# A fused pair of decoder blocks on one core: the opening rearranged into quarters of 256 features

## The reference, cut to what matters

```python
mod_x = split(silu(c) @ w_ada + b_ada, 6)           # shift and gain rows for the tokens: sh1, sc1, ...
mod_c = split(silu(c_ctx) @ w_ada[:, :2*D] + ..., 2) # the same for the context tokens
hx = rms_norm(x, norm1) * (1 + sc1) + sh1            # 256 x 1024
hc = rms_norm(ctx, norm1) * (1 + mod_c[1]) + mod_c[0]
ak, av, gk, gv, lrf, lrb, aq, gq, go, ga, gg = split(hx @ w_in)      # products with slices of w_in
ak_c, av_c, gk_c, gv_c, lrf_c, lrb_c = split(hc @ w_in[:, :CTX_COLS])
```

## Time and profile before

| | |
|---|---|
| time, median of 3 (lowest to highest) | 910.68 us (909.92 to 911.31) |
| profiled execution: its own time, its span | 910.58 us, 908.7 us |
| mean granted TensorE clock | 0.998 |
| PE busy | 889.8 us (98%) |
| DVE busy | 623.5 us (69%) |
| ACT busy | 479.5 us (53%) |
| DMA | 162.11 MB, 178 GB/s in the mean |

### The profile page before, as it was taken

The page is one execution under the profiler, slowest core; times in us unless marked ns, Lnnn a source line. Parts: engine busy times, 40 slices in busy tenths (PEclk is TensorE's granted clock), DMA queues, the critical chain, the costliest instruction groups (busy, mean ns, idle before and its releaser), DMA issues.

```text
span 908.7 us, 14136 instructions
## 1 busy us (share of the span) xinstructions
PE 889.8 (98%) x5128; PEld 761.3 (84%) x5128; DVE 623.5 (69%) x992; ACT 479.5 (53%) x759; POOL 12.6 (1%) x25
## 2 busy tenths in 40 slices
PE   7999999999999999999999999999999999999996
PEld 2688888887788888889999998997888999999985
DVE  2668779779878978775555558767777855555575
ACT  3737545656656566474444444544655744444454
POOL 0200000000000000000000000000000000000001
PEclk9999999999999999999999999999999999999999
DMA  9955212335446877636555558353434665555531
GB/s 360 351 175 171 80 55 93 95 110 153 154 145 230 263 247 263 213 133 230 187 188 185 185 185 270 101 185 117 162 118 161 228 225 197 191 194 183 189 120 47
DMA packets 45376, 162.11 MB, mean 178 GB/s; under 512 B 5615, under 2 KB 5759, under 8 KB 45328
## 3 DMA queue, kind: packets, MB, share of 16 engines
q1 hardware_dynamic: 42896, 155.73, 51.0%
q0 software_dynamic: 1296, 4.02, 1.6%
q10 hardware_dynamic: 1136, 1.70, 0.5%
HBM read 160.39 MB, written 1.05 MB: 178 GB/s over the span
## 4 chain that ended last, share of the span: by engine, by line
PE 80%; DVE 10%; ACT 4%; DMA 3%; issue 2%; POOL 0%; SPq 0%; POOLq 0%; DVEq 0%; ACTq 0%
PE bank L704 67%; DVE w_lo L1706 3%; DMA arena<-in_early 2%; PE bank L971 1%; PE bank L888 1%; ACT w_hi L1271 1%; PE bank L878 1%; ACT arena L1350 1%; PE bank L1173 1%; PE bank L991 1%; PE bank L986 1%; PE bank L1204 1%; DVE small L1736 1%; DMA raw<-in_stream 1%; PE bank L895 1%
## 5 line engine op out<-in xcount | busy, mean ns | idle before, releaser
L1706 DVE TENSOR_TENSOR w_lo<-raw,w_hi 128x1024 fp32r<-128x1024 f32 x244 | 288.0, 1219 | 156.0 <-ACT w_hi L1271 155.3
L1271 ACT ACTIVATE w_hi<-raw 128x1024 fp32r<-128x1024 f32 x244 | 245.2, 1050 | 195.4 <-PE bank L704 163.8
L704 PE MATMUL bank<-w_hi,act_lo 128*128 128x512 f32 (+1 forms) x728 | 294.1, 404 | 0.3 <-DVE w_lo L1706 0.2
L704 PE MATMUL bank<-w_lo,act_hi 128*128 128x512 f32 (+1 forms) x728 | 282.7, 388 | 0.0
L704 PE MATMUL bank<-w_hi,act_hi 128*128 128x512 f32 (+1 forms) x728 | 282.3, 388 | 0.0
L704 PE MATMUL bank<-act_lo,w_hi 128*128 128x256 f32 x640 | 183.0, 286 | 1.1 <-DVE act_lo L1706 0.6
L704 PE MATMUL bank<-act_hi,w_hi 128*128 128x256 f32 x640 | 181.0, 283 | 0.0
L704 PE MATMUL bank<-act_hi,w_lo 128*128 128x256 f32 x640 | 181.0, 283 | 0.0
L704 PEld LDWEIGHTS bank<-w_lo,act_hi 128*128 128x128 f32 x728 | 136.7, 188 | 29.2
L704 PEld LDWEIGHTS bank<-w_hi,act_lo 128*128 128x128 f32 x728 | 137.1, 188 | 26.6 <-issue 1.7
L704 PEld LDWEIGHTS bank<-w_hi,act_hi 128*128 128x128 f32 x728 | 137.2, 188 | 25.8 <-issue 1.2
(11 more groups left out here) (253 smaller groups left out, 768.7 us busy)
## 6 DMA issues: line engine op xcount, KB each, us to landing
raw<-in_stream SPq DMA_DIRECT2D x278, 512.0 KB, 4.4
arena<-in_early SPq DMA_DIRECT2D x14, 512.0 KB, 12.0
res<-in_x ACTq DMA_DIRECT2D x1, 1024.0 KB, 9.0
raw<-in_early SPq DMA_DIRECT2D x2, 512.0 KB, 13.6
arena<-in_ctx SPq DMA_DIRECT2D x1, 1024.0 KB, 13.5
res<-in_x POOLq DMA_DIRECT2D x1, 1024.0 KB, 7.9
arena<-in_norm_final POOLq DMA_DIRECT2D x1, 512.0 KB, 4.1
arena<-in_ple_b POOLq DMA_DIRECT2D x1, 512.0 KB, 5.0
```

Of the source, the lines that this page charges most:

```text
L704: last = pe.matmul(o, left, right, start=start and m == 0, stop=stop and m == 2, skip_group_check=shared)
L1271: return act.activation(o, i, ACT.Copy)
L1706: return dve.tensor_tensor(o, x, hi.bitcast(F32), ALU.subtract)
```

## The change

The opening goes by quarters of 256 features. Early units are laid out anew: four units a quarter, each 512 rows x 256 columns, of shift columns or gain columns. A unit is now four matmuls of 256 columns, one in each strip (step `strip`), before two of 512 in two strips. Per quarter q: four `strip` steps, `flip` (the turn of the tokens' two blocks of 128 features, 4 transposes of 128x128), `row`, `columns` (now 4 transposes of 128x128 instead of products with a strip matrix, which is gone), `mods` (now with a small reduction over the strips by VectorE), `raise` (gain and shift of 128x256 on each of ScalarE and VectorE, then the rounding to `act_hi`), `lower` (`act_lo`), and the gk and gq products of these features, in pieces of 6 matmuls: 24 for gk and 24 for gq a quarter.

In the list of tiles gq and gk change places, so that kv takes gq's slot and its units can be rounded once gq's products are done. gq's second group, which stood behind lr, is now in the quarters; gk of the context and lr come after them. ada 6 stood in front of kv in the stream of raw units and in the steps; it now comes after kv's four units. The context's squares are split in two steps. SP's queue is written by hand up to unit 7, and x comes through it, first, in two halves. The ring of early units is 7 slots, before 7 and two raw buffers.

```diff
-MIXER1 = ["gk", "gq", "kv", ...
+MIXER1 = ["gq", "gk", "kv", ...
-EARLY = (0, 2, 1, 3)
+RING = (1, 4, 5, 6, 7, 8, 0)
@@ mixer1_plan
-    p = Plan([("early",), ("norm", "n0"), ("row", 0), ("row", 1), ("mods", 0), ("turn", "n0", (0, 1))] + cuts("gk", (0, 1))
...
-    p.steps += p.group("gk", 2) + [("evac", "gk", 2), ("prepare",), ("mm", "gk", 3, 0), ("ada", 6, 0), ("mm", "gk", 3, 1),
-                                   ("ada", 6, 1), ("mm", "gk", 3, 2), ("ada", 6, 2), ("mm", "gk", 3, 3), ("evac", "gk", 3),
-                                   ("ada", 6, 3)]
-    p.steps += [("mm", "lr", 0, 0), ("round", "kv", 0), ("cut", "kv", 0), ("evac", "lr", 0), ("round", "kv", 1),
-                ("cut", "kv", 1), ("mm", "gq", 1, 0), ("gate", 0), ("round", "kv", 2), ("mm", "gq", 1, 1), ("log_decay", 0),
-                ("cut", "kv", 2), ("round", "kv", 3), ("mm", "gq", 1, 2), ("cut", "kv", 3), ("mm", "gq", 1, 3),
-                ("evac", "gq", 1)]
+    bring = lambda q: [("row", q), ("columns", q), ("mods", q)]
+    p = Plan([("early",), ("norm", "n0")] + strip(0, 1, 2, 3) + [("flip", 0)] + bring(0) + [("round", "gk", 0), ("raise", 0),
+              ("cut", "gk", 0), ("lower", 0)] + cut("gq", 0)
+             + both("gk", 0, 0) + strip(4, 5) + [("flip", 1)] + both("gk", 1, 0) + strip(6, 7) + cut("gk", 1)
+             + [("row", 1)] + mm("gq", 0, 0, 0) + [("columns", 1), ("mods", 1), ("raise", 1), ("lower", 1)]
+             + mm("gq", 0, 0, 1) + both("gq", 1, 0) + cut("gq", 1))
...
+    p.steps += (both("gk", 0, 2) + [("squares", "n1", 0)] + strip(12, 13) + [("flip", 3)] + both("gk", 1, 2) + cut("gk", 3)
+                + [("squares", "n1", 1)] + strip(14) + mm("gq", 0, 2, 0) + [("norm", "n1")] + strip(15) + [("row", 3)]
+                + mm("gq", 0, 2, 1) + [("columns", 3), ("mods", 3), ("raise", 3), ("lower", 3)] + both("gq", 1, 2)
+                + cut("gq", 3))
+    p.steps += (both("gk", 0, 3) + [("evac", "gk", 0), ("turn", "n1", (0, 1))] + both("gk", 1, 3) + [("evac", "gk", 1)]
+                + [("turn", "n1", (2, 3))] + both("gq", 0, 3) + [("evac", "gq", 0)] + both("gq", 1, 3) + [("evac", "gq", 1)])
+    sides = [[], [("prepare",)], cut("kv", 0), [("evac", "gk", 2)] + cut("kv", 1), [("evac", "lr", 0)] + cut("kv", 2),
+             [("gate", 0)] + cut("kv", 3), [("ada", 6, 0)], [("log_decay", 0), ("ada", 6, 1)], [("evac", "gk", 3)]]
+    for step, side in zip(p.group("gk", 2) + [("mm", "lr", 0, 0)] + p.group("gk", 3), sides):
+        p.steps += [step] + side
+    p.steps += [("ada", 6, j) for j in (2, 3)]
@@ TensorE
+            def strip(p):
+                part, unit = p % 4, early_unit(p).rearrange("p (k n) -> p k n", k=4)
+                half = slice(T * (part % 2), T * (part % 2) + T)
...
+                pe.wait_ge(ada_in[p], 16)
+                for k in range(4):
+                    last = pe.matmul(psum[6][32 * k:32 * k + 32, half], silu_m[:, 4 * (part // 2) + k, :], unit[:, k, :],
+                                     start=(part == 0), stop=(part >= 2), skip_group_check=True)
+                last.then_inc(strips_done, 1)
+            def columns(q):
...
+                for b in range(4):
+                    c = q * NC + b * P
+                    last = pe.transpose(psum[7][:, b * P:(b + 1) * P], ada_row[:, c:c + P], ident)
+                last.then_inc(row_turned, 1)
@@ VectorE
+                elif kind == "raise":
...
+                    dve.wait_ge(turned, q + 1)
+                    dve.tensor_scalar(turn_y[:, q].rearrange("p k t -> p (k t)")[:, 0:T], psum[4][:, 0:T],
+                                      gain[:, 2 * q:2 * q + 1], shift[:, 2 * q:2 * q + 1], ALU.mult, ALU.add).then_inc(turn_y_dve, 1)
+                elif kind == "lower":
...
+                    dve.wait_ge(turn_hi, q + 1)
+                    lo_part(act_lo[:, 2 * q:2 * q + 2, 0:T], ...).then_inc(turn_done, 1)
@@ SyncE
-            for p in range(EARLY_UNITS):
-                if p >= 9:
-                    sp.wait_ge(strips_done, p - 8)
-                sp.dma_start(early_unit(p), a["early"][p]).then_inc(ada_in[p], 16)
...
+            for t in range(TT):
+                sp.dma_start(res[:, t, :], tokens("x")[:, t]).then_inc(x_in[t], 16)
+            for p in range(4):
+                early(p)
+            for u in range(3):
+                unit(u)
+            for p in range(4, 8):
+                early(p)
+            unit(3)
+            unit(4)
+            for p in range(8, 12):
+                early(p)
+            context(0)
+            unit(5)
+            unit(6)
+            context(1)
+            for p in range(12, 16):
+                early(p)
+            unit(7)
```

More of the change, by code:

```diff
@@ new lines, in mixer1_plan @@
+    p.steps += (both("gk", 0, 1) + strip(8, 9) + [("flip", 2)] + both("gk", 1, 1) + strip(10, 11) + cut("gk", 2)
+                + [("row", 2)] + mm("gq", 0, 1, 0) + [("columns", 2), ("mods", 2), ("raise", 2), ("lower", 2)]
+                + mm("gq", 0, 1, 1) + both("gq", 1, 1) + cut("gq", 2))
+    p.steps += (both("gk", 0, 2) + [("squares", "n1", 0)] + strip(12, 13) + [("flip", 3)] + both("gk", 1, 2) + cut("gk", 3)
+                + [("squares", "n1", 1)] + strip(14) + mm("gq", 0, 2, 0) + [("norm", "n1")] + strip(15) + [("row", 3)]
+                + mm("gq", 0, 2, 1) + [("columns", 3), ("mods", 3), ("raise", 3), ("lower", 3)] + both("gq", 1, 2)
+                + cut("gq", 3))
@@ new lines, in flip @@
+            def flip(q):
+                if q == 0:
+                    pe.wait_ge(first_in, 16 * N_FIRST)
+                    pe.wait_ge(norm_ready, TT)
+                for c in range(2):
+                    if q > 0:
+                        pe.wait_ge(turn_y_act if c else turn_y_dve, q)
+                    for t in range(TT):
+                        last = pe.transpose(psum[4 + c][:, t * P:(t + 1) * P], x_norm[:, t, (2 * q + c) * P:(2 * q + c + 1) * P],
+                                            ident)
+                last.then_inc(turned, 1)
@@ L1223, in _ @@
                     mm(*step[1:])
-                elif kind == "early":
-                    early()
+                elif kind == "strip":
+                    strip(step[1])
+                elif kind == "flip":
+                    flip(step[1])
                 elif kind == "columns":
                     columns(step[1])
-                elif kind == "turn" and step[1] != "n0":
+                elif kind == "turn":
                     turn(*step[1:])
@@ L1828, in turn @@
                     ins.then_inc(turn_y_dve, 1)
-                    if name == "n0" and b == 2:
-                        split_unit("gk", 2)
                     if name == "n2" and b == 0:
@@ L2300, in _ @@
                     evac(step[1], step[2])
-                elif kind == "cut" and step[1:] != ("gk", 2):
+                elif kind == "cut":
                     split_unit(step[1], step[2])
@@ L2327, in _ @@
                 elif kind == "mods":
[L2328 to L2330 removed]
+                    q = step[1]
+                    at = slice(2 * q, 2 * q + 2)
+                    if q == 0:
                         dve.wait_ge(first_in, 16 * N_FIRST)
[L2332 removed]
+                    dve.wait_ge(row_turned, q + 1)
+                    sums = stat[:, 7, 8:16].rearrange("p (a c v) -> p a c v", a=2, c=2)
@@ L2453, in laid_out @@
     units = [parts[n][j] for n, j in CUTS]
-    early = [parts[f"ada{i}"][j] for i in EARLY for j in range(4)]
+    early = []
+    for q in range(4):
+        for rows in (0, NC):
+            for c in (T * q, D + T * q):
+                w = inp["w_ada"][0][rows:rows + NC, c:c + T].reshape(4, P, T).transpose(1, 0, 2)
+                early.append(w.reshape(P, 4 * T))
     def columns(v):
```

202 lines of the change are left out of this document (105 added, 97 removed), and 3 rows, old and new, of the table p.

## The result

The changed kernel takes 918.11 us (median, 916.50 to 918.85), the kernel before 910.30 beside it: a ratio of 1.0082, 95% interval [1.0070, 1.0095]. It is slower by 0.8%, outside the 0.2% that the prediction took as no change, and 4.1 us above the forecast of 914.0; the upper end of the range, 918.0, is just missed. The profiled execution took 916.50 us, its span is 914.7. A second profile of the same changed kernel (first experiment) has a span of 916.1, so two executions are read here.

What follows compares the result with a forecast made beforehand. TensorE, busy 98% of the span, was taken as the bound. The opening seemed to give 1.8 us at kv, but VectorE's chain delays the scans, making it 910.6 + 3.4 = 914.0 us; range 908.6 to 918.0.

Steps and rivals of the forecast that it cites:

- Step 1: Landing of early data: 1.33 us per 512 KB, last early unit in at 38.9 us, before about 30.
- step 2: First gk/gq product of the opening: at 17.0 us against 28.59 before, TensorE waiting from 13.5.
- Step 3: Quarters on TensorE: 9.6 us each, quarter 3 begins at 47.5, gk and gq done at 56.1; TensorE paces, not the stream.
- wait for `lower`: In each quarter TensorE waits 0.5 us for VectorE's `lower`; 0.7 more in the third quarter.
- slow start: After the early gap, TensorE's first products run at half pace for a while: 1.0 us more.
- Step 4: From the quarters to the scans: scans at 78.4, 3.2 us later; TensorE idles some 5 us, end moves 3.2 to 3.5.
- cover of tile 6: Before, ada 6's eight VectorE passes ran under gk of the context and lr; claimed gone, scans 3.2 us later.
- TensorE slows again after its wait at L971: Rival: the 5 us wait at the first level product brings half pace, adding 1.5 us: 915.5 to 916; chance 0.15.
- Stream pace: Rival: transfers pace the quarters, quarter 3 begins at 43.3, scans at 73.6; 908.9 us and a little under; chance 0.18.
- Strips not side by side: Rival: strip units take 1.0 instead of 0.5 us, or TensorE stays slow: 6 us more, 920; chance 0.08.
- No change: Rival: gk and gq done at 53 to 54.5 us, total 910.7 to 912.2; chance 0.17.

Runs made afterwards that it cites:

- first experiment: The changed kernel run once more, unedited, beside the kernel before: 918.21 us, ratio 1.0091.
- run with ten products at the level: Changed kernel with ten useless float32 matmuls of 512 columns on TensorE ahead of its wait at the first level product: 918.77 us, ratio 1.0092.
- experiment with five products: Changed kernel with five useless float32 matmuls of 512 columns on TensorE ahead of its wait at the first level product: 916.02 us, ratio 1.0058.

## Why the prediction was wrong

*Step 1 and step 2 held.* First product at 16.63, and at 16.56 to 17.65 in other executions; 17.0 was forecast. The reduction took 0.19 us (0.25 taken, between bounds of 0.17 and 0.69), `raise` 0.54 on VectorE and 0.56 on ScalarE (0.47).

*Step 3 held in its parts.* A quarter at the full clock took 9.86 us (9.6 forecast), the third 10.9 (10.3), the wait for `lower` 0.63 (0.5), a strip unit 0.5 once the clock was full. TensorE set the pace, not the stream. The slow start was in the sum with 1.0; it measured 1.6 and 1.4 in the two profiles after (first quarter 11.43 and 11.24 us against 9.86), and up to 2.7 in other executions (12.53, in the run with ten products at the level). gk and gq were done at 56.4. The forecast of 56.1 was near by some luck: the prediction's own terms give 47.5 + 8.0 = 55.5, and the 0.6 added to it has no term.

*Step 4 held.* Scans at 78.79 (78.4), TensorE's wait 5.16 (some 5), gk's last context group over at about 72 (ScalarE takes it at 72.14), so kv's first product there (71.5), level 1 at 83.18 and 83.77 (82.8). The cover of tile 6 was indeed gone. What I had not seen is that the cover was there to be had: 7.3 us of idle VectorE stood in front of the late steps, and the run with the steps put between the cuts used it.

*The step that failed is the last sentence of step 4 and the sum made from it:* "The kernel has no slack behind it, so the end moves by the same 3.2 to 3.5." The end moved by 6.0 and 7.4 us. A wait of that size was priced at its length only. The runs showed 1.5 to 2.4 us more behind it (first to second level product 6.09, 7.01, 6.98 and 6.57 us in the four profiles that have the wait of 5.2 us, 4.5 to 4.6 in the nine that don't). I had this as a rival, "TensorE slows again after its wait at L971", with the right size for the milder execution (1.5) and too small a chance (0.15).

By the Trainium skill, "TensorE: Matmul & The Clock Gate", section "HAM oscillation — how this bites in real kernels", a wait within a kernel throttles the array again and the work behind it runs at half rate. By this rule, the trace after agrees: 0.50 behind both long waits. The experiment with five products agrees as well, since it left the wait's cause alone and took only the idleness away.

*The rest of the miss* is two smaller terms. The level product stood 0.4 and 1.0 later than forecast: the fourth quarter began at 48.83 instead of 47.5 in the first profile (0.3 more in a quarter, 0.6 in the third, 0.6 at the slow start), took 7.6 instead of 8.0, and from there everything ran as worked out (22.4 us to the scans, 22.3 forecast). And 1.3 us at the turn of y in both profiles after, of which nothing stood in the sum; its cause, transfers that land late, is seen in the profiles, but what makes them late stays open, and the kernel before shows 0.45 of it in one of two profiles.

*The rivals.* Stream pace: refuted, quarters 9.9 and not under 8.5 apart, and shortening the products shortened the quarter. Strips not side by side: refuted, 1.07 for two units of four matmuls. No change: refuted as stated, but near the truth for the opening taken by itself, as the run with tile 6 between the cuts shows (1.0005).

## What to carry to other kernels

When steps are moved out of a stretch in which their engine is idle, look whether there is idle time on the same engine where they go; here four steps placed behind the cuts cost up to 7.6 us, and between the cuts nothing that can be told from the kernel before. Price a wait of TensorE in the middle of a kernel at its length and, where it is several microseconds, at the half pace behind it too: 3.1 us of waiting cost 1.4 to 2.5 more here (first quarters of 11.24 to 12.36 us against 9.86), 5.2 us 1.5 to 2.4 more. Useless products in such a wait pay only if they end before the wait does.

## What the runs showed of the hardware

Waits of 3.13 and 5.16 us brought the granted clock to 0.50; behind waits of 0.55 to 1.84 us it stayed at 1.00 in all profiles. When it falls differs between executions. Behind the first wait in the first profile after, TensorE worked again from 16.63, and the row 17 to 18 still shows 1.00, the next 0.51. With tile 6 ahead of kv it fell during the same wait: 0.85 from 15 to 16, 0.50 from 16 to 17, the first product at 16.95. At the level it fell before the wait ended in both profiles of the changed kernel (0.94 from 82 to 83 in the first, 0.51 from 82 to 84 in the second).

The column of the granted clock can miss a slow stretch near the start. In the run with five products it shows 1.00 from 0 to 24, and the first product lasts 0.58 instead of 0.39 and the first quarter 11.8 us instead of 9.86; in the kernel before, strips of 1064 ns stand at a clock of 1.00. Durations of one kind of matmul tell more there than the column. In that run the four transposes ahead of the wait take 1.06 us, where the first profile after has 0.66: TensorE was slow already when the wait began, so its long first quarter, and the 12.53 us of the run with ten products (1.06 too), are not the price of the wait alone.

Two executions of the changed kernel differ by 0.9 us between the two level products (6.09 and 7.01), out of the 1.4 us between their spans. That this makes the rest of the kernel's spread (916.50 to 918.85) too is not shown: the mean granted clock of its runs doesn't go with their times (0.994 at 918.85, 0.991 at 918.04).
